# Rotation, key split and gate norm moved into the input projections, a symmetric Fourier step, and neighbourhood scores taken from 64 rows

## The reference

```
y_a = fourier_mix(p[..., COL_FOURIER:COL_FOURIER + gw])            # real part of a 2-D FFT over tokens and 64 channels
y_b = neighbourhood_attention(q, k, v, na_kc, na_vc, na_rpb[l], rows)   # 4 heads of 64, bias by offset, masked window
y_c = spatial_gating(p[..., COL_SGU:COL_SGU + 2 * gw], ...)        # gelu; u * (w_s @ layer_norm(v) + b_s)
o_d = diff_latent(q, k, v, df_kc, df_vc, lam, cos, sin)            # 4 heads, two softmaxes of 32 rotated channels each,
y_d = diff_post(o_d, diff_subln_g[l], lam_init)                    #   p = softmax(s1) - lam * softmax(s2)
y = jnp.concatenate([y_a, y_b, y_c, y_d], axis=-1) @ w_out[l]
```

## Time and profile before

| | us |
|---|---|
| median of three runs | 3068.29 |
| lowest and highest run | 3055.95, 3068.49 |
| the profiled execution | 3062.02 |
| its span, first to last instruction | 3060.4 |

### The profile page before, as it was taken

One profiled execution on the slowest core, in us unless ns is written; L12 is line 12 of the kernel. 1 busy time (PEld: TensorE's weight loads), 2 busy tenths in 40 slices (PEclk: granted clock), 3 DMA queues, 4 the chain that ended last, 5 costly groups with the idle time before them and its releaser, 6 DMA issues.

```text
span 3060.4 us, 39832 instructions
## 1 busy us (share of the span) xinstructions
PE 2931.8 (96%) x15873; PEld 2503.1 (82%) x15873; DVE 1688.0 (55%) x2280; ACT 988.0 (32%) x1367; POOL 106.5 (3%) x150
## 2 busy tenths in 40 slices
PE   6999999999999999999888999999999988899999
PEld 5888787979788888789777888888888967788887
DVE  5656655454556676464486555455555248554444
ACT  3333333232333222322265232122223226433222
POOL 0000000000001100000000000000000000000000
PEclk8999999999999999999979999999999999999999
DMA  6333344535234544233430213223322142122332
GB/s 236 115 123 114 113 152 139 173 111 164 73 117 124 180 147 131 97 100 97 110 84 15 83 35 96 85 84 91 101 76 83 56 114 53 56 74 86 103 105 73
DMA packets 269999, 319.00 MB, mean 104 GB/s; under 512 B 25323, under 2 KB 236667, under 8 KB 269852
## 3 DMA queue, kind: packets, MB, share of 16 engines
q1 hardware_dynamic: 243676, 232.83, 24.8%
q0 software_dynamic: 19456, 72.00, 7.7%
q10 hardware_dynamic: 6720, 12.06, 1.2%
HBM read 294.05 MB, written 11.27 MB: 100 GB/s over the span
## 4 chain that ended last, share of the span: by engine, by line
PE 83%; DVE 6%; ACT 3%; DVEq 2%; SPq 2%; issue 1%; DMA 1%; ACTq 0%
PE psum L593 24%; PE psum L594 24%; PE psum L595 24%; PE psum L989 2%; SPq L549 2%; PE psum L759 1%; PE psum L805 1%; PE psum L1001 1%; DVE n_t L1808 1%; DVE w_lo L1820 1%; DVE dneg L2296 1%; DMA ada<-in_w_ada 1%; PE psum L873 1%; DVEq L1807 1%; DVE sba L2307 1%
## 5 line engine op out<-in xcount | busy, mean ns | idle before, releaser
L1820 DVE TENSOR_TENSOR w_lo<-raw,w_hi 128x2048 fp32r<-128x2048 f32 (+1 forms) x244 | 435.3, 1784 | 421.7 <-ACT w_hi L1209 311.5
L593 PE MATMUL psum<-hs_hi,w_hi 128*128 128x512 f32 x1632 | 648.8, 398 | 14.8 <-DVE hs_lo L1812 5.7
L595 PE MATMUL psum<-hs_lo,w_hi 128*128 128x512 f32 x1632 | 638.8, 391 | 0.0
L594 PE MATMUL psum<-hs_hi,w_lo 128*128 128x512 f32 x1632 | 638.7, 391 | 0.0
L593 PEld LDWEIGHTS psum<-hs_hi,w_hi 128*128 128x128 f32 x1632 | 308.2, 189 | 89.5 <-issue 13.3
L595 PEld LDWEIGHTS psum<-hs_lo,w_hi 128*128 128x128 f32 x1632 | 308.2, 189 | 65.7
L594 PEld LDWEIGHTS psum<-hs_hi,w_lo 128*128 128x128 f32 x1632 | 308.7, 189 | 62.7 <-issue 1.2
L1874 DVE SCALAR_TENSOR_TENSOR ada_acc<-ada_raw,csil,ada_acc 128x512 f32<-128x512 f32 x392 | 279.7, 749 | 45.1 <-DMA ada_raw<-in_w_ada 25.7
L593 PE MATMUL psum<-mid_hi,w_hi 128*128 128x512 f32 x768 | 300.5, 391 | 0.0
L594 PE MATMUL psum<-mid_hi,w_lo 128*128 128x512 f32 x768 | 299.7, 390 | 0.0
L595 PE MATMUL psum<-mid_lo,w_hi 128*128 128x512 f32 x768 | 299.3, 390 | 0.0
(11 more groups left out here) (354 smaller groups left out, 4610.7 us busy)
## 6 DMA issues: line engine op xcount, KB each, us to landing
raw<-in_w_in SPq DMA_DIRECT2D x56, 1024.0 KB, 5.2
ada_raw<-in_ada_w POOLq DMA_DIRECT2D x96, 512.0 KB, 4.3
raw<-in_w_ff SPq DMA_DIRECT2D x48, 1024.0 KB, 5.5
raw<-in_w_ff SPq DMA_DIRECT2D x96, 512.0 KB, 3.4
ada_raw<-in_w_ada POOLq DMA_DIRECT2D x32, 512.0 KB, 4.8
raw<-in_w_in SPq DMA_DIRECT2D x24, 512.0 KB, 4.7
ada<-in_w_ada SPq DMA_DIRECT2D x4, 2048.0 KB, 18.8
raw<-in_w_ret_out SPq DMA_DIRECT2D x16, 512.0 KB, 3.4
```

The source lines that it names most:

```text
L593: pe.matmul(dst, lhi, rhi, start=start, stop=False)
L594: pe.matmul(dst, llo, rhi, start=False, stop=False)
L595: return pe.matmul(dst, lhi, rlo, start=False, stop=stop)
L1820: dve.tensor_tensor(w_lo[par][:, 0:kt], raw[par][:, 0:kt], w_hi[par][:, 0:kt].bitcast(F32), ALU.subtract).then_inc(lo_done, 1)
```

## The change

1. **Order of the units.** `COLUMN = [0, 6, 7, 5, 4, 8, 1, 2, 3]`: Fourier, differential q and k, the gate's second and first half, differential v, and last the neighbourhood q, k and v.
2. **Inside the units.** `rotm`, `rope2` and the gate's constants are loaded after unit 4. PE issues one rotation product behind each of units 4 to 7, all into one bank. DVE rotates (`rotate`), splits (`split`), and takes the gate's statistics and norm (`gate_stats`, `gate_norm`) between its weight splits; ACT rounds `dfqc` and `dfq` there. The last rotation, the rounding of k and its split come behind the units.
3. **Stacking.** The 16 copies of q start before the last product ends. k and its context lie side by side (`dfk_all`), so 16 copies of 768 columns take the place of 32.
4. **Symmetric transform.** `dft` is loaded for 257 of 512 token frequencies. PE computes the cosine part for 257 and the sine part for 255 columns, side by side in one bank; ACT copies both out, and DVE adds and subtracts them with a reversed write (`mirrored`) inside the first three differential items. The gate's product now stands ahead of the transform.
5. **64 rows.** The neighbourhood scores read 64 partitions of `naq_hi`, `naq_lo`, `nak_hi`, `nak_lo` directly. The zero tiles, their memsets and the eight (layer 1: four) small copies and subtractions per layer are gone; ACT and DVE treat `naq` (and `naqc`) once as a whole.

```diff
@@ SP
-                    load(n + j, (n + j) % 2, cols(win2[l], 256 * j))
-                sp.wait_ge(gemm_done, R(n + 9))
-                sp.dma_start(cc[:], d["cc"]).then_inc(cc_in, 16)
...
+                    load(n + j, (n + j) % 2, cols(win2[l], 256 * COLUMN[j]))
+                    if j == 4:
+                        sp.wait_ge(gemm_done, R(n + 2))
+                        sp.dma_start(rotm[:], d["rotm"]).then_inc(rope2_in, 16)
+                        sp.dma_start(rope2[:], d["rope2"]).then_inc(rope2_in, 16)
...
-                sp.wait_ge(df_split, 4 * l + 3)
+                sp.wait_ge(lo_done, n + 9)
+                sp.wait_ge(df_split, 2 if l == 0 else 4)
                 for a in range(2):
                     for half in range(2):
-                        stack(ks, 0, S, dfk_hi, (0, 1), a, half, stacked[a])
-                        stack(ks, 0, S, dfk_lo, (2, 3), a, half, stacked[a])
                         stack(qs, 0, S, dfq_hi, (0, 2), a, half, stacked[a])
                         stack(qs, 0, S, dfq_lo, (1, 3), a, half, stacked[a])
-                        stack(ks, S, SC, dfkc_hi, (0, 1), a, half, stacked[a])
-                        stack(ks, S, SC, dfkc_lo, (2, 3), a, half, stacked[a])
+                sp.wait_ge(gemm_done, R(n + 9))
+                sp.dma_start(cc[:], d["cc"]).then_inc(cc_in, 16)
+                sp.dma_start(ws[:], d["sgu_w_2"][l].rearrange("g p q -> p g q")).then_inc(ws_in, 16)
...
+                sp.wait_ge(df_split, 3 if l == 0 else 5)
+                for a in range(2):
+                    for half in range(2):
+                        stack(ks, 0, S + SC, dfk_hi_all, (0, 1), a, half, stacked[a])
+                        stack(ks, 0, S + SC, dfk_lo_all, (2, 3), a, half, stacked[a])
@@ PE, units
+                    if 4 <= u < 8:
+                        j = u - 4
...
+                            pe.wait_ge(rot_read, 4 * l + j)
+                        pe.matmul(X0[:], rotm[:], (dfq, dfk)[j // 2][:, j % 2, :], start=True, stop=True).then_inc(rot_done, 1)
@@ PE, transform
+                for c in range(2):
+                    for half, (a_, b_, n0_, n1_) in enumerate(((0, 257, 0, 257), (257, 512, 1, 256))):
+                        for t in range(4):
+                            mm = pe.matmul((X0, X1)[c][:, a_:b_], u_f[:, t, c, half * P:(half + 1) * P], dft[:, half, t, n0_:n1_],
+                                           start=t == 0, stop=t == 3)
+                    mm.then_inc(f2_done, 1)
@@ PE, neighbourhood scores
-                    q_hi, q_lo = (z[it.head % 2][:, c, tok] for z in (qz_hi, qz_lo))
+                    rows = slice(HD * (it.head % 2), HD * (it.head % 2 + 1))
+                    q_hi, q_lo = (z[rows, c, tok] for z in ((naqc_hi, naqc_lo) if it.ctx else (naq_hi, naq_lo)))
                     if not it.ctx:
-                        product(dst[:, 0:S], q_hi, q_lo, nak_hi[:, c, :], nak_lo[:, c, :], True, True)
+                        product(dst[:, 0:S], q_hi, q_lo, nak_hi[rows, c, :], nak_lo[rows, c, :], True, True)
@@ ACT, behind the units
+                act.wait_ge(rot_read, 4 * l + 4)
+                act.copy(dfk_hi_all[:], dfk_all[:]).then_inc(df_hi, 1)
@@ DVE
+                rotate(3)
+                split(2 if wc else 1, dfk_all, dfk_lo_all, dfk_hi_all)
                 if wc:
                     ada_take2(23, 1)
...
-                for z in (*qz_hi, *qz_lo):
-                    dve.memset(z[:].bitcast(F32), 0.0).then_inc(qz_zero, 1)
...
+                    if i < T // 2:
+                        dve.wait_ge(f2_read, 3 * l + i + 1)
+                        if i < 2:
+                            mirrored(y_fo[:, i], f_odd[:, i, 0:255], 256)
```

More of the change, by code:

```diff
@@ L104, in unit_plan @@
     return first, results, with_ctx
+COLUMN = [0, 6, 7, 5, 4, 8, 1, 2, 3]
 def ada_starts():
@@ L308, in build @@
-        dfk_hi = at("dfk_hi", [P, 2, S], F32R, H0 + 43008)
+        rotm = at("rotm", [P, P], F32, Q2 + 41120)
+        rot_t = at("rot_t", [P, S], F32, Q2 + 41632)
+        f_odd = at("f_odd", [P, 3, S // 2], F32, H0 + 12288)
+        dfk_hi_all = at("dfk_hi_all", [P, 2, S + SC], F32R, H0 + 43008)
         sbb = [at("sbb0", [P, 768], F32, H0 + 25600), at("sbb1", [P, 768], F32, Q2 + 41120)]
         na_bias = at("na_bias", [P, 4, NB_DR - 1, GRID], F32, H0 + 28672)
-        qz_hi = [at(f"qz_hi{i}", [P, 2, S], F32R, H0 + 4096 * i) for i in range(2)]
@@ L1045, in _ @@
                     mm.then_inc(f1_done, 1)
-                if wc:
-                    pe.wait_ge(x_scaled, 1)
-                for j in range(4):
-                    src = (dfq, dfk)[j // 2]
-                    pe.matmul((X0, X1, C0, C1)[j][:], rotm[:], src[:, j % 2, :], start=True, stop=True).then_inc(rot_done, 1)
                 pe.wait_ge(ws_in, 16 * (l + 1))
@@ L1084, in _ @@
                         mm.then_inc(sg_done, 1)
+                pe.wait_ge(dft_in, 32 * (l + 1))
+                pe.wait_ge(rot_read, 4 * l + 4)
+                for c in range(2):
[4 more added lines that the diff above has]
+                    mm.then_inc(f2_done, 1)
+                if wc:
+                    for c in range(2):
+                        for half, (a_, b_, n0_, n1_) in enumerate(((0, 129, 0, 257), (129, 256, 2, 256))):
+                            for t in range(2):
+                                mm = pe.matmul(C0[:, 256 * c + a_:256 * c + b_], u_f[:, 4 + t, c, half * P:(half + 1) * P],
+                                               dft[:, half, t, n0_:n1_:2], start=t == 0, stop=t == 1)
+                    mm.then_inc(f2_done, 1)
                 pe.wait_ge(sg_out, 3 * l + T // 2)
@@ L1127, in na_score @@
                     dst = S3[i % 2]
-                    if it.pos == 0:
-                        pe.wait_ge(nqz_ready, g0 + it.group + 1)
+                    if it.pos == 0 and it.head == 0:
+                        pe.wait_ge(nq_split, 2 * l + (2 if it.ctx else 1))
                     if i < 2:
@@ L1635, in df_exps @@
                                        accum_out=dden[:, it.group % 2, half, it.pos:it.pos + 1]).then_inc(done, 1)
-                def nqz_his(it):
-                    r_ = slice(HD * (it.head % 2), HD * (it.head % 2 + 1))
-                    act.copy(qz_hi[it.head % 2][r_, it.head // 2, 0:SC if it.ctx else S],
-                             (naqc if it.ctx else naq)[r_, it.head // 2, :]).then_inc(nqzhi_done, 1)
                 df_exps(0, its[0])
@@ L1669, in _ @@
                         na_exps(i + 1, its[i + 1])
-                    if its[i].pos == its[i].size - 1 and its[i].group + 4 < len(first_of):
-                        nqz_his(first_of[its[i].group + 4])
                     take_pt(i, its[i], na_t, na_pt, na_pv)
@@ L2235, in _ @@
                         ada_part("w_in_0", u)
-                dve.wait_ge(psum_free, R(n + 6))
-                for t in range(T):
-                    dve.bn_stats(ln_st[:, t, :], sgu[:, t, GW:2 * GW])
-                dve.drain()
-                for t in range(T):
-                    last = dve.bn_aggr(ln_mv[:, t, :], ln_st[:, t, :])
-                last.then_inc(mv_ready, 1)
+                    if u == 4:
+                        gate_stats()
+                    elif u == 5:
+                        rotate(0)
+                        if wc:
+                            split(0, dfqc, dfqc_lo, dfqc_hi)
+                    elif u == 6:
+                        rotate(1)
+                        gate_norm()
+                    elif u == 7:
+                        rotate(2)
+                        split(1 if wc else 0, dfq, dfq_lo, dfq_hi)
@@ L2404, in _ @@
                         na_max(i + 2, its[i + 2])
-                    if its[i].pos == its[i].size - 1 and its[i].group + 4 < len(first_of):
-                        nqz_los(first_of[its[i].group + 4])
                     if i == 6:
```

214 lines of the change are left out of this document (108 added, 106 removed).

## The result

The changed kernel takes 3124.36 us (median; 3121.42 to 3130.28), the kernel before 3065.96 us beside it. The ratio is 1.0197, with a 95% interval of 1.0181 to 1.0214: the change makes the kernel **2% slower**. The profiled execution took 3124.72 us, its span is 3123.1 us, and its mean granted clock is 0.943. The forecast was 3113 us, with a range of 3066 to 3142.

A forecast was written before the change was run, and what follows sets the result against it. PE, busy for 96% of the span, was taken to bound the kernel. From 3062.0 us, 25.6 gained in steps 1 to 4 and 76.5 lost in step 5 gave 3113 us, range 3066 to 3142.

The forecast's parts named there:

- Step 1: Layer 0, up to the first differential scores: 8.5 us gained net, after 1.6 us of extra wait for the modulation result.
- Step 2: Layer 1, up to the differential scores: 12.8 us gained net, plus 1.0 for four memsets ahead of the first maximum.
- Step 3: Start of the second head in differential attention: DVE's waits go, 5.1 us gained in layer 0, 2.7 in layer 1.
- Step 4: Differential stage: mirrored additions cost DVE 2.2 and 1.4 us, ACT's rounding of naq 0.5 and 0.4 (layers 0, 1).
- Step 5: Neighbourhood scores from 64 rows: both stages run at half clock, 72.5 us lost, plus 4 for the switch.
- the switch: Neighbourhood items: going between 128-row and 64-row products costs about 0.09 us, in and out of 40 items; 4 us taken.
- The credit of 4 us: Neighbourhood stage of layer 1: it begins at full clock, so 4 us is taken off its loss, leaving 32.
- Part of a stage: Rival: only one layer, or part of a neighbourhood stage, falls to half clock; about 40 us lost, 3076 us; chance 0.11.
- The clock does not care for rows: Rival: 64 rows do not lower the neighbourhood clock, only the switch costs 4 to 7 us; 3041 us; chance 0.16.

The follow-up runs named there:

- experiment 10: Experiment 3's kernel with the last modulation result taken on DVE before the key split instead of behind it; 3041.94 us, ratio 0.9929.
- experiment 8: Experiment 3's kernel with the transform at full width again, without sine part or mirrored additions; 3047.74 us, ratio 0.9933.
- experiments 2: Changed kernel with neighbourhood scores over all 128 rows, queries not zeroed, so two heads' scores are mixed; 3038.64 us, ratio 0.9909.
- experiment 3: Changed kernel with correct neighbourhood scores from 128 rows, queries multiplied by 1 or 0 by row; 3037.70 us, ratio 0.9921.
- experiment 9: Experiment 3's kernel with each key copy made in two pieces again, 16 instead of 8 for each head; 3029.63 us, ratio 0.9888.
- experiments 1: Kernel before the change, with only the neighbourhood score products reading the 64 rows of their own head; 3157.93 us, ratio 1.0317.
- experiments 6: Changed kernel with each large neighbourhood item's grid-key and context-key products alternating between the two 64-row groups; 3066.66 us.
- experiment 7: Changed kernel with the scores of two neighbouring items issued together, in turn from the two 64-row groups; 3086.43 us.
- experiment 5: Kernel before the change, with 64-row scores in one of four large neighbourhood items, 8 of 40; 3068.67 us.

## Why the prediction was right

Sign and mechanism were right: the neighbourhood stages run at half clock because their scores use 64 rows. The time was 11 us low (3113 against 3124). The loss was put 14 us too small and the gains 4 us too small, so one miss hid a part of the other.

*Step 1, layer 0.* The first differential scores came 8.5 us earlier, as forecast, with no DMA ahead of them. The wait for the modulation result is 2.34 us where the DMA wait had been 0.96, so 1.4 extra where I took 1.6, and experiment 10 shows its cause. The exact hit is luck in part: the channel transform starts 3.6 us later, where I had 5.0 (1.6 of wait and 3.4 of rotation), and from there to the scores it is 25.5 us, where my terms give 24.1. Also, over the kernels with this layout and the half-width transform the stretch from channel transform to scores is 22.7 to 30.0 us, since TensorE's clock falls to half in it in some of them (below).

*Step 2, layer 1.* From channel transform to scores the gain is 15.6 us, against 15.8 by my terms (16.2 less 0.4). From the transposes of y 0 to the channel transform it is 0.7 us less instead of 3.0 more; over the kernels here with the changed units this stretch is 788.8 to 797.9 us, so that is not a term of its own. The half transform was shown by itself in experiment 8. That experiment also contradicts one reason in this step: the wait for the table did not go because the table is half the size. And the 15.6 us hold only where the clock does: in experiments 2 and 3 the same stretch takes 22.3 and 22.2 us, a gain of 10.6 or so.

*Step 3, the second head.* In layer 0 the waits of 3.40 and 1.74 us are gone: the maxima of the second head follow without a bracket. I had given the fewer copies as the reason. Experiment 9 contradicts that: with 16 key copies for each pair of heads instead of 8 the scores are no later. It is the start of the copies that counts: the first key copy is issued at 1489.09 in the changed kernel, beside the channel transform, where it was 1504.83, 19 us behind it. In layer 1 DVE had waited 2.08 and 0.99 us there and now waits 0.61 and 1.49, so 1.0 us came of the 2.7 that I took.

*Step 4, the additions.* On DVE, behind the first mix of layer 0:

```profile
1520.97 0.41 DVE L2284 TENSOR_TENSOR y_fo<-y_fo,f_odd 128x255 f32<-128x255 f32 x1
1521.31 0.42 DVE L2285 TENSOR_TENSOR y_fo<-y_fo,f_odd 128x255 f32<-128x255 f32 x1
1521.64 1.75 DVE L2330 TENSOR_REDUCE dneg<-psum 128x2 f32<-128x1536 f32 x1
```

They cost 0.34 and 0.33 us from start to start, as priced; writing in reverse order costs nothing. Over the whole differential stage layer 0 gained 4.4 us (2.4 forecast) and layer 1 0.6 (1.9 net). In layer 1 the clock fell to half for 6.8 us, from 2549.8, at the place of the waits of 0.61 and 1.49 us; the wait at the end of the stage is 1.80 us, where it was 1.50.

*Step 5, the rows.* **This step decided, and both of its terms were too small.** The clock did what the step said, and experiments 1 to 3 show that the rows did it. Why unused rows weigh on the clock stays open: experiments 6 and 7 do not settle it. The item was mis-sized: 5.78 us is an item of 128 rows at half clock, and the switch came on top of it, 0.47 us by the rows of after where I had 0.1 (4 us over 40 items). By measured numbers it is 6.25 - 3.10 = 3.15 us an item instead of 2.7 and 0.1. Layer 0 lost 47.4 us against 40.7 and a share of the 4, layer 1 43.1 against 32. The credit of 4 us for a start at full clock in layer 1 was wrong as well: of its stage only 5.6 us ran at 2.4 GHz, with PE busy for 3.8 of them, and from the first scores to the first values it is 9.1 us instead of 7.0 (in layer 0 11.0 instead of 8.0). The last items of layer 1, which have no scores beside them, follow by 4.99 us instead of 3.10: 5.7 us in three steps, where I had 1.2 in two. Together 90.5 instead of 76.5. The other steps gave 29.6 instead of 25.6. That makes 10.0 of the 11.8 us by which the profiled execution is over the sum (3124.72 against 3112.9); the other 1.8 lie behind the last matmul.

*The rivals.* "Part of a stage" did not happen; that the clock can hold with fewer such items is what experiment 5 shows, with 8 of 40. "The clock does not care for rows" fell in experiments 1 and 2; its time of 3041 is what experiment 3 measures (3038), for the reason that the rows are back. The rule of the Trainium skill that step 5 cites (idle gaps bring the clock down, rows not at all) does not cover this case: in the changed kernel PE is busy for 98.77 of 102.40 us at 0.50.

## What to carry to other kernels

Slicing a contraction to the rows that hold data saved nothing where products ran one after another. Each was as long as with all rows. Going to 64 rows and back cost 0.28 us an item at 2.4 GHz. And a stage in which such products took about a third of the time (2.22 of 6.25 us an item) ran at half of its clock with PE busy for 97.39 of 102.80 us. Padding with zeros to all rows, by folding a 0/1 column into an operation that is needed anyway, gave the clock back in both layers. Issuing products of different row groups in turn, so that they run side by side, made them shorter in both layers and kept the clock in one of two. Check the granted clock of the stage, not the busy share. When a wait for copies is to go, look at when the first one is issued before counting them.

## What was not expected

- Products of 64 rows on different row groups can start within 0.01 us of each other, with nothing asked for but the partitions of their operands. Two of 512 columns take 0.43 us at 1.2 GHz together, like one (experiment 7, 1614.51 to 1614.94).
- The level at which a stage began went with the level that it kept: with two row groups in turn layer 1 held 2.4 GHz (0.99) and layer 0, entered at 1.2, stayed at 0.50 for 115 us with the same kind of items.
- The transform's stretch, now shorter and with waits of 0.7 to 0.8 us at three places, is a place where the clock falls in some kernels and not in others. Two kernels that differ only in the key copies, layer 1, from channel transform to scores (experiment 3, then experiment 9):

```profile
2461.00:2483.30 22.30, 19.99 (x84) 0.77 0.84 197
```

```profile
2460.40:2477.70 17.30, 15.08 (x84) 1.00 0.79 200
```

The same 84 matmuls take 5.0 us longer at a clock of 0.77. Why it falls in the one and not in the other was not settled, since each was traced once; differences of 5 us between kernels of this family should not be read as effects of an edit. For that reason I do not call experiment 9 faster than experiment 3.
